# Two dense MLPs and two SwiGLU feed-forwards on one core: a reciprocal, down blocks, weight splits and parts of x in another order

## The chip, the cores and the metric

The kernel runs on one core of one Trainium2 chip. The metric is the device time of one execution in microseconds (us); the number compared is the median of several runs. TensorE (PE) multiplies, VectorE (DVE) and ScalarE (ACT) work on the tiles, GpSimd (POOL) adds and issues a few transfers, and SyncE (SP) issues nearly all of them.

## What is computed

Everything is float32, for 512 tokens of 1024 features. Two transformer blocks come first (stick-breaking attention, then retention, each with an MLP behind it), then a third block whose feed-forwards stand ahead of and behind a mixer of sparse attention and mLSTM:

```python
for layer in range(2):
    h = h + mixer(rms_norm(h, g_mix[layer]))            # stick-breaking, then retention
    u = relu(rms_norm(h, g_mlp[layer]) @ w_mlp_up[layer])   # 1024 -> 4096
    h = h + (u * u) @ w_mlp_down[layer]                 # 4096 -> 1024
x = rms_norm(h, g_final)
# second block, D_FF = 2816
x = x + 0.5 * (silu(n(x) @ w_gate) * (n(x) @ w_up)) @ w_down    # ffn1
x = x + mix(rms_norm(x, mix_norm)) @ w_out
x = x + 0.5 * (silu(n(x) @ w_gate) * (n(x) @ w_up)) @ w_down    # ffn2
```

Retention splits its projection into q and k (256 a head), v and a gate (512 a head) and scales the value rows by 1/rms of their token.

## The kernel before, in words

**Precision.** Each float32 factor is split in two numbers that TensorE takes at full rate: `w_hi` is a rounded copy by ScalarE (`split_hi`, L835), `w_lo = raw - w_hi` by VectorE (`split_lo`, L1684), and likewise `x_hi`/`x_lo` and `u_hi`/`u_lo`. A product is three matmuls: w_hi with x_hi, w_hi with x_lo, w_lo with x_hi.

**Blocks.** A weight block is 1024 by 128, read by one 512 KB transfer into one of two `raw` slots. Block n uses slot n % 2 of `raw`, `w_hi` and `w_lo`, and a PSUM bank. TensorE starts block n when `hi_done` says that w_hi is there and `bank_free` that the bank's last product was read; 16 matmuls with w_hi (L2834) are followed by 8 with w_lo (L2839). w_hi of block n + 2 can be made when block n is done (`mm_done`), and block n + 2 is loaded when split_lo(n) has read the slot (`lo_done`).

**MLPs (layers 0 and 1).** The first 8 up blocks are dense (`mlp`, c = 0 to 7). VectorE reads the product into `u_act` (L2034), which frees its bank; ScalarE squares it and makes `u_hi`; VectorE makes `u_lo`. The factor 1/rms isn't in u: it is squared (`inv_sq`) and multiplied in with the down products. Besides, each c makes parts for later: `x_forms` are sums and differences of halves of x (`x_sum`, split into `xs_hi`, `xs_lo`).

**Pairs.** The other up columns, and in layers 2 and 3 (ffn1, ffn2) gate and up, are made in pairs of blocks by a Strassen-like scheme of 7 units (q, p), p = 1 to 7, each 12 matmuls of 256 columns (L3133 with the high part of a form, L3137 with the low). The forms of pair q lie in `forms[q % 2]`: four transfers by SP (`load_forms`, L746, L749, L752, L755), a fifth by GpSimd that adds a block onto two of them (L2790), and two sums by VectorE (`third_form` L1942, `fourth_form` L1947). `form_high` (L1037) and `form_low` (L1935) split each form into a ring of four. Units 1 and 6 are copied by ScalarE (`first_copy`, `second_copy`, L1044); unit 4 adds onto the bank of 7 and waits until `last_copy` (L2075) has read it. `up_phase` sets the order of the units: in the first phase of a feed-forward it is (q0,5), (q0,1), (q0,2), (q0,6), (q0,7), (q1,1), (q0,4), (q0,3), (q1,2), (q1,6), ... Units 1, 2 and 4 read x itself; in layers 2 and 3 that is the normed x, in four parts, which `x_normed_high` (L1215) and `x_normed_low` (L2176) write over `x_hi` and `x_lo` once the last dense block has read them.

**Down blocks.** The hidden chunks are taken in groups of 8 (in a feed-forward 8, 8, 6). `up_and_down` lays the first two down blocks n and n + 1 of a group among the last units, chunk by chunk as u becomes ready (`down_part`, L3146); the other six follow as dense blocks (`run`).

**Queues.** Every engine works through its own list in the order of the code; SP does too, so a transfer waits for those written ahead of it. At the start TensorE turns x into columns, with 24 empty transposes (`keep_awake`) in between.

## Time and profile before

| | us |
|---|---|
| median of 3 runs | 2423.54 (2421.94 to 2423.86) |
| the profiled execution, its own time | 2422.37 |
| its span, first to last instruction | 2420.5 |
| PE busy | 2397.0 (99%) |
| DVE busy | 1625.4 (67%) |
| ACT busy | 1156.2 (48%) |
| POOL busy | 154.7 (6%) |

The chain of work that ended last lies for 90% of the span on PE, and the granted PE clock is full in each of the 40 slices of the page. So the time changes only where PE's idle time does: a row's bracket, [idle before <-releaser], says how long an engine was idle ahead of an instruction and what ended it.

### The profile page before, as it was taken

The page shows a single profiled execution, that of the slowest core. Times are in us where ns is not written, and L with a number is a line of the kernel's source. Part 1 is how long each engine was busy: PE and PEld are TensorE (multiplying, and loading weights), DVE is VectorE, ACT ScalarE, POOL GpSimd, SP SyncE. Part 2 cuts the span into 40 slices and gives each one's busy share as a digit, 9 for nine tenths or more (in the row PEclk, how much of TensorE's full clock was granted, in tenths as well). Part 3 has the DMA queues.
Part 4 walks back from the last instruction along what each step waited for, and adds up shares of the span by engine and source line. Part 5 has one row for each costly group of instructions (what it writes and reads, how often), then busy time and mean ns, then how long its engine had stood idle before and what let it go on. Part 6 is the DMA issues. An engine that isn't in the chain of part 4 may idle for free.

```text
span 2420.5 us, 35737 instructions
## 1 busy us (share of the span) xinstructions
PE 2397.0 (99%) x13500; PEld 2063.5 (85%) x13500; DVE 1625.4 (67%) x2386; ACT 1156.2 (48%) x1837; POOL 154.7 (6%) x151
## 2 busy tenths in 40 slices
PE   9999999999999999999999999999999999999999
PEld 7777798998888888789998889898787778889998
DVE  6777765666656646756666967676968846867664
ACT  3565544554343443535645535354465453544443
POOL 2001000001000000100003000002000001000000
PEclk9999999999999999999999999999999999999999
DMA  4212443533222223445541555552222222555552
GB/s 140 68 64 70 148 148 106 156 105 106 95 79 81 76 79 96 134 136 138 149 131 61 158 147 167 139 157 85 79 70 70 70 70 96 151 154 164 142 154 82
DMA packets 108194, 273.50 MB, mean 113 GB/s; under 512 B 15120, under 2 KB 33808, under 8 KB 107920
## 3 DMA queue, kind: packets, MB, share of 16 engines
q1 hardware_dynamic: 95168, 237.98, 29.6%
q0 software_dynamic: 8640, 31.46, 7.8%
q10 hardware_dynamic: 4240, 2.10, 0.3%
q8 instruction: 94, 1.54, 0.3%
q14 instruction: 52, 0.43, 0.1%
HBM read 269.40 MB, written 2.10 MB: 112 GB/s over the span
## 4 chain that ended last, share of the span: by engine, by line
PE 90%; DVE 5%; issue 2%; ACT 1%; DMA 1%; POOL 1%; DVEq 0%; SPq 0%; ACTq 0%; POOLq 0%
PE ps L2834 29%; PE ps L3133 16%; PE ps L2839 14%; PE ps L3137 8%; PE ps L3146 6%; PE ps L3213 4%; PE ps L2887 2%; PE ps L3514 2%; PE ps L2903 2%; PE ps L3256 1%; PE ps L3038 1%; PE ps L3014 1%; PE ps L2991 1%; PE ps L3243 1%; DVE w_lo L1684 1%
## 5 line engine op out<-in xcount | busy, mean ns | idle before, releaser
L835 ACT ACTIVATE w_hi<-raw 128x1024 fp32r<-128x1024 f32 x286 | 302.4, 1059 | 771.2 <-PE ps L2839 584.5
L1684 DVE TENSOR_TENSOR w_lo<-raw,w_hi 128x1024 fp32r<-128x1024 f32 x286 | 352.1, 1231 | 118.5 <-ACT w_hi L835 118.1
L2834 PE MATMUL ps<-x_hi,w_hi 128*128 128x512 f32 x848 | 337.4, 398 | 4.8 <-DVE u_act L2034 4.4
L2834 PE MATMUL ps<-x_lo,w_hi 128*128 128x512 f32 x848 | 330.6, 390 | 0.0
L2834 PE MATMUL ps<-u_hi,w_hi 128*128 128x512 f32 x642 | 250.8, 391 | 2.8 <-ACT w_hi L835 2.8
L2834 PE MATMUL ps<-u_lo,w_hi 128*128 128x512 f32 x642 | 249.9, 389 | 0.0
L3133 PE MATMUL ps<-xs_hi,ring 128*128 128x256 f32 x960 | 240.8, 283 | 1.3 <-ACT second_copy L1044 1.3
L3133 PE MATMUL ps<-xs_lo,ring 128*128 128x256 f32 x960 | 240.7, 283 | 0.0
L1037 ACT ACTIVATE ring<-forms 128x512 fp32r<-128x512 f32 x300 | 187.7, 628 | 87.8 <-PE ps L3137 85.8
L2839 PE MATMUL ps<-x_hi,w_lo 128*128 128x512 f32 x848 | 209.5, 389 | 0.0
L2834 PEld LDWEIGHTS ps<-x_hi,w_hi 128*128 128x128 f32 x848 | 159.2, 188 | 45.6 <-issue 11.0
L2834 PEld LDWEIGHTS ps<-x_lo,w_hi 128*128 128x128 f32 x848 | 159.3, 188 | 33.5 <-issue 1.7
L2839 PEld LDWEIGHTS ps<-x_hi,w_lo 128*128 128x128 f32 x848 | 159.2, 188 | 33.1
L3133 PEld LDWEIGHTS ps<-xs_hi,ring 128*128 128x128 f32 x960 | 184.2, 192 | 1.7 <-issue 1.7
L3133 PE MATMUL ps<-x_hi,ring 128*128 128x256 f32 x720 | 180.9, 284 | 3.6 <-DVE x_lo L2176 1.8
L3133 PEld LDWEIGHTS ps<-xs_lo,ring 128*128 128x128 f32 x960 | 184.3, 192 | 0.1
L3133 PE MATMUL ps<-x_lo,ring 128*128 128x256 f32 x720 | 180.6, 283 | 0.0
L2839 PE MATMUL ps<-u_hi,w_lo 128*128 128x512 f32 x642 | 159.0, 389 | 0.0
L1935 DVE TENSOR_TENSOR ring_b<-forms,ring 128x512 fp32r<-128x512 f32 x224 | 152.3, 682 | 4.1 <-ACT ring L1037 3.9
L2834 PEld LDWEIGHTS ps<-u_hi,w_hi 128*128 128x128 f32 x642 | 120.5, 188 | 29.7 <-DVE h L1837 4.9
L3133 PEld LDWEIGHTS ps<-x_hi,ring 128*128 128x128 f32 x720 | 138.0, 192 | 5.5 <-issue 3.0
L1837 DVE SCALAR_TENSOR_TENSOR h<-ps,h 128x512 f32<-128x512 f32 (+1 forms) x71 | 49.0, 690 | 138.7 <-PE ps L2839 116.4
(476 smaller groups left out, 4653.5 us busy)
## 6 DMA issues: line engine op xcount, KB each, us to landing
raw<-in_stream SPq DMA_DIRECT2D x293, 512.0 KB, 3.6
forms<-in_stream SPq DMA_DIRECT2D x180, 256.0 KB, 4.4
forms<-in_stream SPq DMA_DIRECT2D x60, 512.0 KB, 4.7
forms<-in_stream POOLq DMA_DIRECT2D x60, 512.0 KB, 5.7
x_tok<-in_x SPq DMA_DIRECT2D x4, 512.0 KB, 8.0
out_x<-xn ACTq DMA_DIRECT2D x7, 256.0 KB, 2.3
tab_ret<-in_tables_ret SPq DMA_DIRECT2D x1, 1536.0 KB, 6.6
raw<-in_stream SPq DMA_DIRECT2D x3, 256.0 KB, 3.2
```

The source lines that it names most:

```text
L835: nc.scalar.activation(w_hi[:, slot(n)], raw[:, slot(n)], ACT.Copy).then_inc(hi_done, 1)
L1037: nc.scalar.activation(form_hi[form_slot(v)], form_of(q, p), ACT.Copy).then_inc(flag("f_hi"), 1)
L1684: nc.vector.tensor_tensor(w_lo[:, slot(n)], raw[:, slot(n)], w_hi[:, slot(n)].bitcast(F32), ALU.subtract).then_inc(lo_done, 1)
L1837: nc.vector.scalar_tensor_tensor(out=dst, in0=product(n), scalar=scale, in1=dst, op0=ALU.mult, op1=ALU.add).then_inc(bank_free[slot(n)], 1)
L1935: nc.vector.tensor_tensor(form_lo[form_slot(v)], form_of(q, p), form_hi[form_slot(v)].bitcast(F32), ALU.subtract).then_inc(flag("f_lo"), 1)
L2834: nc.tensor.matmul(ps[:, gemm_bank(n)], w_hi[:, s, k], x(k), start=(k == 0 and i == 0), stop=False)
L2839: last = nc.tensor.matmul(ps[:, gemm_bank(n)], w_lo[:, s, k], hi(k), start=False, stop=(k == kc - 1))
L2887: return nc.tensor.transpose(dst, src, ident)
L3133: nc.tensor.matmul(bank, form_hi[s][:, j * P:(j + 1) * P], x_part(p, j, i == 0), start=(p in (1, 2, 5) and j == 0 and i == 0), stop=False, ...
L3137: last = nc.tensor.matmul(bank, form_lo[s][:, j * P:(j + 1) * P], x_part(p, j, True), start=False, stop=(j == 3), skip_group_check=True)
L3146: last = nc.tensor.matmul(ps[:, gemm_bank(n)], w[:, slot(n), k], x[:, 0, k], start=(k == 0 and i == 0), stop=(k == kc - 1 and i == 2))
L3213: return nc.tensor.matmul(ps[:, RET_BANKS[tb]], x[:, c, tb * P:(tb + 1) * P], weights, start=(c == 0 and w is w_hi and x is x_hi), stop=(c ...
```

## The change

It has seven parts: (1) the reciprocal of an MLP's norm, and its square, are made behind up block 5 instead of block 0; (2) at the end of each group of a feed-forward, PE finishes down block n ahead of all chunks from 4 on of block n + 1; (3) the splits of these two blocks' weights, ahead of units (q0,3) and (q1,6) before, stand at (q1,6) and (q2,6), and one set of forms is loaded between the loads n and n + 1; (4) VectorE makes the first three low parts of the normed x ahead of the fourth low form and `fourth_form`, and ScalarE the fourth high part at unit 5 instead of unit 6; (5) retention's first value block waits for `first + 2` and `first + 3` in place of `first + 4` and `first + 5`; (6) the first gains are loaded by ScalarE's queue; (7) ScalarE splits weight block 0 ahead of the second chunk of x.

```diff
@@ SP, start
             load_x(0)
-            sp.dma_start(prm[:, 0:DC], params[:, 0:DC]).then_inc(sig("gain_in"), 16)
             load_values(0)
@@ SP, load_layer
                     load(n)
+                    if layer >= 2 and g == 0:
+                        load_forms(qs[1] + 2)
                     load(n + 1)
                     for q in qs:
-                        if q + 2 < PAIR_FROM[layer + 1] and (layer < 2 or g or q > qs[0]):
+                        if q + 2 < PAIR_FROM[layer + 1] and (layer < 2 or g or q > qs[1]):
                             load_forms(q + 2)
@@ ACT, start
+            nc.scalar.dma_start(prm[:, 0:DC], params[:, 0:DC]).then_inc(sig("gain_in"), 16)
             nc.scalar.preload_act_table_set("sqrt_and_others")
             act.wait_ge(sig("gain_in"), 16)
             high_of(N_MIX0, 0)
+            split_hi(0)
             high_of(N_MIX0, 1)
-            split_hi(0)
@@ ACT, gate_pairs
-                    if g == 0 and (q, p) == (qs[0], 6):
+                    if g == 0 and (q, p) == (qs[0], 5):
                         x_normed_high(layer, 3)
...
-                    if g == 0 and (q, p) in ((qs[0], 3), (qs[1], 6)):
-                        split_hi(RUN_AT[LAYERS[layer]] + 2 * FFN_DENSE + q - qs[0])
+                    if g == 0 and (q, p) in ((qs[1], 6), (qs[2], 6)):
+                        split_hi(RUN_AT[LAYERS[layer]] + 2 * FFN_DENSE + q - qs[1])
@@ DVE, mlp
                     split_lo(n + 2)
-                    if c == 0:
-                        inverse(norm)
-                        nc.vector.tensor_tensor(inv_sq[:], inv[:], inv[:], ALU.mult).then_inc(flag("down_scaled"), 2)
                     dve.wait_ge(sig("uh_done"), chunks_before + c + 1)
                     nc.vector.tensor_tensor(u_lo[:, 0, c], u[:, c % 2], u_hi[:, 0, c].bitcast(F32),
                                             ALU.subtract).then_inc(sig("ul_done"), 1)
+                    if c == 5:
+                        inverse(norm)
+                        nc.vector.tensor_tensor(inv_sq[:], inv[:], inv[:], ALU.mult).then_inc(flag("down_scaled"), 2)
@@ DVE, gate_pairs
-                    if g == 0 and (q, p) in ((qs[0], 3), (qs[1], 6)):
-                        split_lo(RUN_AT[LAYERS[layer]] + 2 * FFN_DENSE + q - qs[0])
+                    if g == 0 and (q, p) in ((qs[1], 6), (qs[2], 6)):
+                        split_lo(RUN_AT[LAYERS[layer]] + 2 * FFN_DENSE + q - qs[1])
@@ DVE, ffn
                         third_form(PAIR_FROM[layer])
-                        form_low(v)
-                        form_low(v + 1)
-                        fourth_form(PAIR_FROM[layer])
-                        form_low(v + 2)
-                        form_low(v + 3)
+                        for i in range(3):
+                            form_low(v + i)
                         for i in range(3):
                             x_normed_low(layer, i)
+                        form_low(v + 3)
+                        fourth_form(PAIR_FROM[layer])
@@ PE, up_and_down
                     if layer < 2:
                         down_part(n, made, (kc - 2,), kc)
-                    else:
-                        down_part(n + 1, made, range(4, kc - 1), kc)
                     down_part(n, made, (kc - 1,), kc)
-                    down_part(n + 1, made, range(4 if layer < 2 else kc - 1, kc), kc)
+                    down_part(n + 1, made, range(4, kc), kc)
@@ PE, retention
-            pe.wait_ge(bank_free[0], turn(first + 4, 1))
-            pe.wait_ge(bank_free[1], turn(first + 5, 1))
+            pe.wait_ge(bank_free[0], turn(first + 2, 1))
+            pe.wait_ge(bank_free[1], turn(first + 3, 1))
```

Each value block waits besides, in `r_value_block`, for `bank_free` of its own slot: the first for `turn(first + 4, 1)`, the second for `turn(first + 5, 1)`. These lines are not changed.

On VectorE, in the MLP of layer 0, between up blocks 0 and 1, the kernel before has this:

```order
L2034 TENSOR_SCALAR u_act<-ps 128x512
L1684 TENSOR_TENSOR w_lo<-raw,w_hi 128x1024
L1719 RECIPROCAL inv<-std 128x512
L2038 TENSOR_TENSOR inv_sq<-inv 128x512
L2040 TENSOR_TENSOR u_lo<-u,u_hi 128x512
L1878 TENSOR_TENSOR xs_lo<-x_sum,xs_hi 128x1024
```

With the change these two instructions stand at the end of block 5 (lines are those of the changed file):

```order
L2036 TENSOR_SCALAR u_act<-ps 128x512
L1686 TENSOR_TENSOR w_lo<-raw,w_hi 128x1024
L2039 TENSOR_TENSOR u_lo<-u,u_hi 128x512
L1721 RECIPROCAL inv<-std 128x512
L2043 TENSOR_TENSOR inv_sq<-inv 128x512
L2036 TENSOR_SCALAR u_act<-ps 128x512
```

So nothing stands any more between w_lo and u_lo of block 0, and the two instructions stand ahead of the read of block 6.

On TensorE, at the end of the first group of layer 2, the kernel before goes, ahead of the dense down blocks (the group of four is chunks 0 to 3 of block n + 1):

```order
L3146 MATMUL ps<-u_hi,w_lo 128x512 x4
L3146 MATMUL ps<-u_hi,w_hi 128x512 x3
L3146 MATMUL ps<-u_lo,w_hi 128x512 x3
L3146 MATMUL ps<-u_hi,w_lo 128x512 x3
L3146 MATMUL ps<-u_hi,w_hi 128x512
L3146 MATMUL ps<-u_lo,w_hi 128x512
L3146 MATMUL ps<-u_hi,w_lo 128x512
L3146 MATMUL ps<-u_hi,w_hi 128x512
L3146 MATMUL ps<-u_lo,w_hi 128x512
L3146 MATMUL ps<-u_hi,w_lo 128x512
```

And with the change:

```order
L3147 MATMUL ps<-u_hi,w_lo 128x512 x4
L3147 MATMUL ps<-u_hi,w_hi 128x512
L3147 MATMUL ps<-u_lo,w_hi 128x512
L3147 MATMUL ps<-u_hi,w_lo 128x512
L3147 MATMUL ps<-u_hi,w_hi 128x512 x4
L3147 MATMUL ps<-u_lo,w_hi 128x512 x4
L3147 MATMUL ps<-u_hi,w_lo 128x512 x4
```

Before, three chunks of block n + 1 (9 matmuls), the last chunk of block n (3) and the last of block n + 1 (3); now the last chunk of block n at once, and four chunks of block n + 1 (12) behind it. In the groups of 6 chunks the 9 matmuls are 3.

On VectorE, at the end of the dense part of layer 2, where the ring gets the first four low forms, the kernel before has:

```order
L1942 TENSOR_TENSOR form_sum<-forms_80 128x512
L1935 TENSOR_TENSOR ring<-forms_80,ring 128x512
L1935 TENSOR_TENSOR ring_b<-forms_80,ring 128x512
L1947 TENSOR_TENSOR form_sum<-forms_80,form_sum 128x512
L1935 TENSOR_TENSOR ring_b<-forms_80,ring 128x512
L1935 TENSOR_TENSOR ring_b<-form_sum,ring 128x512
L2176 TENSOR_TENSOR x_lo<-x_even,x_hi 128x2x256 x2
L2176 TENSOR_TENSOR x_lo<-x_odd,x_hi 128x4x256
L1696 SCALAR_TENSOR_TENSOR u<-ps,inv 128x512
```

With the change:

```order
L1944 TENSOR_TENSOR form_sum<-forms_80 128x512
L1937 TENSOR_TENSOR ring<-forms_80,ring 128x512
L1937 TENSOR_TENSOR ring_b<-forms_80,ring 128x512 x2
L2178 TENSOR_TENSOR x_lo<-x_even,x_hi 128x2x256 x2
L2178 TENSOR_TENSOR x_lo<-x_odd,x_hi 128x4x256
L1937 TENSOR_TENSOR ring_b<-form_sum,ring 128x512
L1949 TENSOR_TENSOR form_sum<-forms_80,form_sum 128x512
L1698 SCALAR_TENSOR_TENSOR u<-ps,inv 128x512
```

The three x_lo instructions moved up past two others; what follows them is where it was.

## Rows read from the trace of the kernel before

**Rows 1.** The page: busy time, share of the span and instructions of each engine

```profile
PE 2397.0 (99%) x13500; PEld 2063.5 (85%) x13500; DVE 1625.4 (67%) x2386; ACT 1156.2 (48%) x1837; POOL 154.7 (6%) x151
```

**Rows 2.** Waits of PE over the span: total us, times, longest

```profile
PE ps L2834 <- DVE u_act L2034: 4.4, 2, 2.3
PE ps L2834 <- ACT w_hi L835: 3.2, 6, 0.6
...
PE ps L3133 <- DVE last_copy L2075: 1.7, 2, 0.9
...
PE ps L3137 <- DVE ring_b L1935: 0.2, 1, 0.2
PE ps L2887 <- DVE h L1837: 0.2, 1, 0.2
```

**Rows 3.** Timeline, MLP of layer 0: start, us, engine, line, tiles, [idle before]

```profile
255.92 3.35 DVE L1719 RECIPROCAL inv<-std 128x512 f32<-128x512 f32 x1 [1.98 <-ACT std L888]
256.44 0.63 ACT L1134 ACTIVATE u_hi<-u 128x512 fp32r<-128x512 f32 x1
...
259.99 0.68 DVE L2040 TENSOR_TENSOR u_lo<-u,u_hi 128x512 fp32r<-128x512 f32 x1
...
265.90 1.97 PE L2839 MATMUL ps<-x_hi,w_lo 128*128 128x512 f32 x8
...
269.32 0.68 DVE L2034 TENSOR_SCALAR u_act<-ps 128x512 f32<-128x512 f32 x1
...
270.15 0.47 PE L2834 MATMUL ps<-x_hi,w_hi 128*128 128x512 f32 x1 [2.28 <-DVE u_act L2034]
```

**Rows 4.** Timeline, the first down block of layer 0: its weights and first matmuls

```profile
288.74 1.06 ACT L835 ACTIVATE w_hi<-raw 128x1024 fp32r<-128x1024 f32 x1 [5.11 <-DMA raw<-in_stream]
...
292.01 1.07 PE L3146 MATMUL ps<-u_hi,w_hi 128*128 128x512 f32 x4
```

**Rows 5.** Timeline of TensorE and VectorE, end of a group in layer 2

```profile
1420.65 0.42 DVE L2083 TENSOR_TENSOR u<-ps,second_copy 128x256 f32<-128x256 f32 x1 [2.58 <-PE ps L3137]
...
1422.50 0.69 DVE L2097 TENSOR_TENSOR u_lo<-u,u_hi 128x512 fp32r<-128x512 f32 x1 [0.70 <-ACT u_hi L1170]
...
1428.09 2.01 ACT L835 ACTIVATE w_hi<-raw 128x1024 fp32r<-128x1024 f32 x2 [5.62 <-PE ps L3146]
...
1429.28 0.49 PE L2834 MATMUL ps<-u_hi,w_hi 128*128 128x512 f32 x1 [0.55 <-ACT w_hi L835]
```

**Rows 6.** Timeline, second pair of layer 2: a weight split and unit 4

```profile
1392.00 1.22 DVE L1684 TENSOR_TENSOR w_lo<-raw,w_hi 128x1024 fp32r<-128x1024 f32 x1
...
1395.50 0.36 PE L3133 MATMUL ps<-x_hi,ring 128*128 128x256 f32 x1 [0.85 <-DVE last_copy L2075]
```

**Rows 7.** Timeline, third pair of layer 2: its last_copy, and a form that waits

```profile
1399.04 0.33 SPq L746 DMA_DIRECT2D forms<-in_stream  x1
...
1404.50 0.42 DVE L2075 COPY last_copy<-ps 128x256 f32<-128x256 f32 x1 [0.75 <-PE ps L3137]
...
1408.52 0.69 DVE L1942 TENSOR_TENSOR form_sum<-forms 128x512 f32<-128x512 f32 x1 [2.54 <-DMA forms<-in_stream]
```

**Rows 8.** Timeline, layer 3, the first parts of the normed x

```profile
2105.94 1.14 ACT L1215 ACTIVATE x_hi<-x_even 128x512 fp32r<-128x512 f32 x2
...
2107.35 0.68 DVE L1935 TENSOR_TENSOR ring_b<-form_sum,ring 128x512 fp32r<-128x512 f32 x1
...
2107.95 1.28 DVE L2176 TENSOR_TENSOR x_lo<-x_even,x_hi 128x512 fp32r<-128x512 f32 x2
...
2108.78 0.36 PE L3133 MATMUL ps<-x_hi,ring 128*128 128x256 f32 x1 [1.53 <-DVE x_lo L2176]
```

**Rows 9.** Timeline, retention: the first value block

```profile
611.13 1.17 PE L3213 MATMUL ps<-w_hi,x_hi 128*128 128x512 f32 x4 [1.09 <-DVE r_x L1696]
```

**Rows 10.** Timeline, the start: the gains' transfer and the first real matmuls

```profile
1.68 0.50 SPq L721 DMA_DIRECT2D prm<-in_params  x1
...
9.60 2.12 PE L2903 MATMUL ps<-w_hi,x_hi 128*128 128x512 f32 x8
```

## The prediction

> **What bounds the kernel now.** I read the page first: PE is busy for 2397.0 us of a span of 2420.5 [rows 1], and the granted clock is full throughout. No work is removed, so at most the idle 23.5 us and what hides beside them are to be had. Then the list of what PE waited for: the reader is to see that few waits are long and that five of them are the subject of the change [rows 2]. Then the timeline around each of these, PE beside VectorE and ScalarE [rows 3 to 9]: which engine is late, and what stands ahead of the late instruction in its list.
>
> One reading is needed for the prices. A row of eight matmuls is 1.97 us long [rows 3] and one alone 0.39, so they start 0.226 apart, and each row covers 0.16 us beyond the next start. In the MLP the last of eight starts at 265.90 + 1.97 - 0.39 = 267.48, the next matmul at 270.15: 2.67, less the normal 0.226, is 2.44 us lost, where the idle column says 2.28 [rows 3]. So a stall costs its idle time plus 0.16. The Trainium skill (Perfetto Trace Analysis, Identifying the Most-Contended Engine) says that matmul occupancy is no good measure for TensorE since its instructions are pipelined. By idle times alone the sum below would be some 2 us smaller; the trace agrees with the page through the 0.16.
>
> **The change part by part.**
>
> (1) Reciprocal in the MLPs. It waits 1.98 us for std and takes 3.35, then the square follows, and only then u_lo of block 0, at 259.99, though its u_hi was there at 256.44 + 0.63 = 257.07 [rows 3]. u_lo moves to 257.1, 2.9 us earlier. Behind it come xs_lo, four sums and the reads of blocks 1 and 2, all VectorE's own chain or ScalarE's answer to it, so the read of block 2 (269.32) starts near 266.45 and ends at 267.1. PE wants that bank at 267.7: the stall goes, with 0.6 to spare. Layer 1 has the second of the two waits of 4.4 us [rows 2], 2.1 idle. Gain 4.4 + 2 x 0.16 = 4.7. The reciprocal's new place: PE wants the bank of block 6 again when block 7 is done, two blocks of 24 x 0.226 = 5.4 us behind block 5. u_lo of block 5 ends about 3 us behind its product (read, square, high and low part at 0.6 to 0.7 each), so 7.8 us are left for reciprocal, square and read, 3.35 + 0.7 + 0.7 = 4.8; hidden. With less cover each missing microsecond would cost one. Next late is the weight of the first down block: w_hi starts on a DMA landing at 288.74 and w_lo is ready some 1.06 + 1.22 later, at 291.0, against PE at 292.01, now 289.5 [rows 4, 6]. Its transfer stands behind eight loads of forms, which stand behind a load that waits for the split of block 5. That split moves 2.9 earlier with the chain, the split of block 6 by about 2.6, and so the transfer by the same; I take slack as kept. The other bound is that it doesn't move at all: 1.6 lost a layer.
>
> (2) End of a feed-forward group. w_hi of block n + 2 can't be made until block n is done; it starts at 1428.09, and PE starts at 1429.28 after 0.55 idle [rows 5]. Of the six waits for w_hi [rows 2] five are at the ends of such groups: four like this one, and that of the group of 6 chunks, which is the longest with 0.6. 4 x 0.55 + 0.6 + 5 x 0.16 = 3.6; the sixth lies elsewhere and stays. Block n is now done 9 matmuls earlier in the groups of 8, 9 x 0.226 = 2.0 us, more than the 0.71; in the group of 6 it is 3 x 0.226 = 0.68 of its 0.77. In the first group of layer 2 the bank comes next: its read stands behind a reciprocal, I leave 0.1 for that. Gain 3.6 - 0.2 = 3.4. The last group ends with PE's wait for h, 0.2 idle [rows 2]; 0.68 is more than its 0.36: gained whole. Together 3.75. What speaks against it: the last chunk's u_lo is now wanted 2.0 us earlier. The last six matmuls and the nine ahead of them begin 14 x 0.226 before 1428.34 (1429.28 less the idle 0.55 and a row of 0.39), at 1425.2; u_lo ends at 1422.50 + 0.69 = 1423.2 [rows 5]. 2.0 us are left, so hidden.
>
> (3) Splits and forms. PE waits 0.85 for last_copy at 1395.50, as VectorE has two weight splits of 1.22 each within four microseconds, one at 1392.00 [rows 6]. The first of them leaves. VectorE has then caught up and is only as late as PE's product of unit 7 allows, which is 0.3 us or more ahead of the wait. Both waits for last_copy go: 1.7 + 2 x 0.16 = 2.0 [rows 2]. The other split goes to the third pair, where last_copy at 1404.50 has 0.75 us idle ahead of it [rows 7] and the ring is ahead: 1.22 against 0.75 makes last_copy 0.5 late, about what lies between last_copy and PE's wait for it. I take nothing; the other bound is 0.5 a layer. SP: a load now waits for the split at the third pair, 84 matmuls of 256 columns behind the one at 1392.00, some 9 us, near 1402.3 at its end, and the forms that had been issued at 1399.04 stand behind it [rows 7], 3.7 us later. That helps the set before, whose added part reached VectorE at 1408.52 only, 2.54 late [rows 7]; PE's 0.2 behind it goes, 0.2 + 0.16 = 0.4. For the later set I reckon its landing at about the old time, since the same bytes wait for fewer; VectorE has 2.58 us idle behind the place where it wants it [rows 5].
>
> (4) x parts. In layer 3 x_hi is there from 2105.94 + 0.57 on (two in 1.14), but x_lo starts at 2107.95 behind two instructions that move behind it, 0.60 start to start each (2107.35 to 2107.95) [rows 8]. 1.2 us earlier is 2106.75, still behind x_hi. PE's 1.53 + 0.16 shrinks by 1.2. In layer 2 VectorE is ready before x_hi, and moving the rest changes nothing. The next four low forms and fourth_form are 1.2 later; the copies behind them wait for PE longer than that. Gain 1.2. ScalarE's fourth part at unit 5 instead of 6 frees second_copy by 0.1 at most: nothing.
>
> (5) Retention. PE waits 1.09 us for r_x [rows 9], the read of block first + 3, but the first value block's own wait asks only for the bank of first + 2, read a block earlier. The wait moves behind 24 matmuls, 5.4 us, and goes: 1.09 + 0.16 = 1.25.
>
> (6, 7) Start. PE works without idle time up to its first real matmuls at 9.60 [rows 10], since the empty transposes end just then; an earlier block 0 gains nothing. SP saves 0.50 us of issue [rows 10]. Between 0 and 0.5 lost if the small transfer on its own queue delays the first ones; I take 0.
>
> Sum: 4.7 + 3.75 + 2.0 + 0.4 + 1.2 + 1.25 = 13.3. The profiled execution took 2422.37, so 2409.1; it lies 1.2 below the median, and 2423.54 - 13.3 = 2410.2.
>
> **The rivals.**
>
> All as summed, 0.66: 2410.2, its own range 2408 to 2412.5.
>
> Down weights late in the MLPs, 0.12. The transfers there are many, and the landing may hold at 288.74 [rows 4]. Then PE, at 289.5, waits until 291.1: 1.6 of layer 0's gain goes and about as much of layer 1's, 2410.2 + 3 = 2413.2. For it: w_hi waits 5.11 us for that DMA. Against: what it waits behind moves with it.
>
> The moved split and the later forms make new stalls, 0.09. 0.3 to 0.5 a layer at the third pair and about 1 a layer where the added form lands beyond the 2.58: 2413.
>
> The gains' transfer delays the start, 0.05. PE's first transposes want the first part of x; if that comes 0.5 later, all does, 2410.7. The Trainium skill (DMA: Bandwidth & Descriptors, Issuing engines are not separate DMA queues; Queues, rings and completion order) says that transfers of all engines share 16 DMA engines, which take turns between queues, and that another queue only saves issue time. No row here shows the split.
>
> The change only hands the stalls on, 0.06. w_hi early but the bank late at group ends, and half of every gain back at the next wait: 2416.9. Against it speak the slacks worked out above, each over 0.3.
>
> Slower than before, 0.02: the forms issued after 1399.04 come so late that the hidden chunk behind third_form stops PE. It decides only once the landing is late by more than VectorE's 2.58, the 2.0 that u_lo has, and half the sum, 6.7, in each of two layers: 11 us, where the issue moves by 3.7. One more microsecond makes 2426.
>
> **Range and chances.** A difference under 0.2%, 4.8 us, can't be told from none here. 2407.5 to 2415 takes in the first four cases with the unknown bounds (0.5 at the start, 0.5 a layer at the splits, 3 at the weights) and leaves out the last two. All but the slower case and the upper half of the fifth lie below 2418.7: faster 0.95, same 0.03, slower 0.02.
>
> **What would show it.** PE's list of waits without u_act, with w_hi at 0.5 us or less in total, last_copy and r_x gone, x_lo at about 0.6; u_lo of block 0 in the MLP right behind its u_hi, the reciprocal behind block 5. PE's idle time near 12 us. Wrong would make it: a wait of PE for w_hi or w_lo of the first down blocks, one for a bank at the group ends, or for u_lo of the last chunk, or the first x later than before.

## The result, and the profile after

| us | before | after |
|---|---|---|
| median, runs of the first comparison | 2423.7 (4: 2421.94 to 2424.52) | 2407.44 (4: 2407.14 to 2407.99) |
| the profiled execution, its own time | 2422.37 | 2407.99 |
| its span | 2420.5 | 2406.2 |

The ratio is 0.9932, interval 0.9918 to 0.9945: faster by 0.7%, that is by 16.3 us in the medians and by 14.4 in the two profiled executions. The forecast was 2410.2, with a range of 2407.5 to 2415.0. The sign and the places were right; the size was 2.8 us short, and the result lies 0.06 us below the range.

The page of the changed kernel, its line of busy times, answers to [rows 1]:

```profile
PE 2393.8 (99%) x13500; PEld 2063.6 (86%) x13500; DVE 1627.7 (68%) x2386; ACT 1157.2 (48%) x1837; POOL 155.1 (6%) x151
```

TensorE is idle for 2406.2 - 2393.8 = 12.4 us, where it was 23.5; the forecast said near 12. Its list of waits (total us, times, longest) answers to [rows 2]:

```profile
PE ps L3134 <- ACT second_copy L1046: 1.1, 2, 0.6
...
PE ps L3134 <- DVE x_lo L2178: 0.6, 2, 0.4
PE ps L2835 <- DVE h L1839: 0.5, 1, 0.5
...
PE ps L2835 <- ACT w_hi L836: 0.3, 1, 0.3
```

The lines of the kernel before that [rows 2] does not show:

```profile
PE ps L3133 <- DVE x_lo L2176: 1.8, 2, 1.5
PE ps L3133 <- ACT second_copy L1044: 1.3, 2, 0.7
...
PE ps L3213 <- DVE r_x L1696: 1.1, 1, 1.1
```

u_act, last_copy, r_x and ring_b are gone, w_hi is down from 3.2 to 0.3, x_lo from 1.8 to 0.6, second_copy from 1.3 to 1.1. New is the 0.5 for a sum of h: one of the forecast's signs of being wrong, a bank that is late at a group end, has come in one group. The MLP of layer 0 (timeline of VectorE and TensorE, against [rows 3]):

```profile
256.67 0.69 DVE L2039 TENSOR_TENSOR u_lo<-u,u_hi 128x512 fp32r<-128x512 f32 x1 [3.17 <-ACT u_hi L1136]
...
260.08 0.68 DVE L2036 TENSOR_SCALAR u_act<-ps 128x512 f32<-128x512 f32 x1
...
265.46 1.98 PE L2840 MATMUL ps<-x_hi,w_lo 128*128 128x512 f32 x8
267.27 0.39 PE L2835 MATMUL ps<-x_hi,w_hi 128*128 128x512 f32 x1
...
281.30 3.35 DVE L1721 RECIPROCAL inv<-std 128x512 f32<-128x512 f32 x1
284.75 0.69 DVE L2043 TENSOR_TENSOR inv_sq<-inv 128x512 f32<-128x512 f32 x1
285.36 0.69 DVE L2036 TENSOR_SCALAR u_act<-ps 128x512 f32<-128x512 f32 x1
```

u_lo of block 0 stands right behind its u_hi, TensorE goes from block to block at 267.27 with no idle time, and the reciprocal in its new place ends, with the read of block 6 behind it, at 286.05. TensorE wants that bank only with the matmul at 289.04, behind the eight that begin at 287.22, so 3.0 us are left, as forecast (7.8 less 4.8).

To see where the time came from I compared, over the whole program, the start of the k-th matmul in both traces. This difference, the lead of the changed kernel, grows in steps: 0.46 us from the first real matmul on, 2.54 and 2.43 in the two MLPs, 1.37 at retention's values, 1.07 and 1.09 at last_copy of layers 2 and 3, 0.48 at the form of layer 2, 0.08 and 1.18 at the x parts, and at the ends of the six groups 0.03, 0.84, 0.67, 0.84, 0.84 and 0.43. Together 14.35.

The end of the first group of layer 2 (timeline, against [rows 5]) has the 0.03:

```profile
1411.65 0.69 DVE L1944 TENSOR_TENSOR form_sum<-forms 128x512 f32<-128x512 f32 x1 [3.52 <-DMA forms<-in_stream]
...
1412.86 0.42 DVE L2085 TENSOR_TENSOR u<-ps,second_copy 128x256 f32<-128x256 f32 x1
...
1415.91 3.35 DVE L1721 RECIPROCAL inv_final<-std_final 128x512 f32<-128x512 f32 x1
...
1417.64 1.06 ACT L836 ACTIVATE w_hi<-raw 128x1024 fp32r<-128x1024 f32 x1 [2.97 <-PE ps L3147]
...
1420.08 0.69 DVE L1839 SCALAR_TENSOR_TENSOR h<-ps,h 128x512 f32<-128x512 f32 x1
...
1420.82 0.50 PE L2835 MATMUL ps<-u_hi,w_hi 128*128 128x512 f32 x1 [0.50 <-DVE h L1839]
```

w_hi is there at 1418.70, two microseconds early, as forecast. But VectorE waited 3.52 us for the late forms, so the reciprocal begins late and the read of the bank behind it ends at 1420.77.

### The profile page after: what moved, and what is told of

Its sections match the earlier page's. It is cut to its first block, busy times and chain, and to the rows that moved or that the text cites. A ratio compares the mean times of both kernels' runs of the same rounds, so it can differ in the third digit from the quotient of the medians.

```text
span 2406.2 us, 35737 instructions
## 1 busy us (share of the span) xinstructions
PE 2393.8 (99%) x13500; PEld 2063.6 (86%) x13500; DVE 1627.7 (68%) x2386; ACT 1157.2 (48%) x1837; POOL 155.1 (6%) x151
## 4 chain that ended last, share of the span: by engine, by line
PE 92%; DVE 4%; issue 2%; ACT 1%; DMA 1%; POOL 1%; SPq 0%; ACTq 0%; DVEq 0%; POOLq 0%
PE ps L2835 29%; PE ps L3134 16%; PE ps L2840 14%; PE ps L3138 8%; PE ps L3147 6%; PE ps L3212 4%; PE ps L3513 2%; PE ps L2904 2%; PE ps L2888 2%; PE ps L3255 1%; PE ps L3039 1%; PE ps L3015 1%; PE ps L2992 1%; PE ps L3242 1%; DMA forms<-in_stream 1%
## 5 line engine op out<-in xcount | busy, mean ns | idle before, releaser
L2840 PEld LDWEIGHTS ps<-u_hi,w_lo 128*128 128x128 f32 x642 | 120.5, 188 | 25.0
L2835 PEld LDWEIGHTS ps<-u_lo,w_hi 128*128 128x128 f32 x642 | 120.5, 188 | 24.9
```

Of the source, the lines that this page charges most:

```text
L2835: nc.tensor.matmul(ps[:, gemm_bank(n)], w_hi[:, s, k], x(k), start=(k == 0 and i == 0), stop=False)
L2840: last = nc.tensor.matmul(ps[:, gemm_bank(n)], w_lo[:, s, k], hi(k), start=False, stop=(k == kc - 1))
```

## Experiments

Times below are medians; where the runs of one kernel fall into groups, the single runs are given. A lead is always that of TensorE over the kernel before, read matmul by matmul from two traces. The kernel before was timed 75 times beside these experiments.

### First set: a control and three parts alone

**e1_null**: no edit but a comment.

> The kernel before, unchanged in every instruction. It measures the measurement: the runs of the kernel before lie between 2421.94 and 2424.52 us, those of the changed one within 0.9 us. Theory A (the trace accounts for 14.3 us of the gain, and the 2 us that the medians show beyond it are scatter of the kernel before from run to run): ratio 1.000 within 0.0006, single runs scattered over some 2.5 us here too. Theory B (the kernel before has, in its other runs, waits that its profiled execution did not have, and the change removes them): the same scatter here, and then a single part below must give more by its timed runs than its two traces account for.

Measured: 2423.06 against 2423.42, ratio 0.9996 (0.9987 to 1.0005), 11 runs from 2421.44 to 2424.20. Each run also has the granted clock of TensorE as a mean over the span: the five fastest have 1.000, the six from 2423.06 on 0.999. The scatter of the kernel before goes with the clock. Its trace also leads that of before, the same kernel, by 0.40 us from the form of layer 2 on and loses 0.33 at a form of layer 3: the wait of 0.2 us for ring_b in [rows 2] is one outcome, not a fixed cost.

**e2_reciprocal**:

```diff
-                    if c == 0:
+                    if c == 5:   # behind u_lo of the block
                         inverse(norm)
                         nc.vector.tensor_tensor(inv_sq[:], inv[:], inv[:], ALU.mult)
```

> Part 1 alone. By the forecast's pricing, a stall costs its idle time plus 0.16 us: 4.7 us. By the traces of before and after, in which the lead of TensorE grows by 2.54 and 2.43 us in the two MLPs, a stall costs its idle time plus 0.27 us: 5.0 us, ratio 0.9979. If the down weights come late (the rival of the forecast) it is 1.6 us less a layer. Waits of TensorE: none for u_act, the rest as before.

Measured: 2417.20 against 2423.42, 6.2 us, ratio 0.9974 (0.9964 to 0.9985). Its trace leads that of before by the expected 2.54 and 2.41 in the MLPs, and by 0.26 at the form of layer 2, which is scatter as in e1. So the timed gain is 1.2 us more than the two steps account for, and the scatter shrinks: 8 runs within 1.3 us, all at a clock of 1.000, where 30 runs of before spread over 3.7.

**e3_down_blocks**:

```diff
-                    if layer < 2:
-                        down_part(n, made, (kc - 2,), kc)
-                    else:
-                        down_part(n + 1, made, range(4, kc - 1), kc)
+                    if layer < 2:
+                        down_part(n, made, (kc - 2,), kc)
                     down_part(n, made, (kc - 1,), kc)
-                    down_part(n + 1, made, range(4 if layer < 2 else kc - 1, kc), kc)
+                    down_part(n + 1, made, range(4, kc), kc)
```

> Part 2 alone. The forecast says 3.75 us. With 0.27 us for a stall in place of 0.16 and with the first group of layer 2 gaining nothing (its bank comes next: with all parts in, TensorE waits there 0.50 us for a sum of h that stands behind a reciprocal) it is 0.84 x 3 + 0.7 + 0.4, about 3.5 us, ratio 0.9986. If parts 3 and 2 depend on each other (the reciprocal's place is set by the read of the pair before), the first group of layer 2 gains here what it did not gain with all parts in: 4.2 us.

Measured: 2419.33, 4.1 us, ratio 0.9982 (0.9973 to 0.9991); steps of the lead 0.64, 0.85, 0.67, 0.84, 0.84, 0.43, so 4.3. The first group of layer 2 gains 0.64 here and 0.03 with all parts in: another part takes it back.

**e4_gains_by_scalar_queue**:

```diff
-            sp.dma_start(prm[:, 0:DC], params[:, 0:DC]).then_inc(sig("gain_in"), 16)
+            nc.scalar.dma_start(prm[:, 0:DC], params[:, 0:DC]).then_inc(sig("gain_in"), 16)
```

> Part 6 alone. In the changed kernel TensorE leads by 0.46 us from its first blocks on; the forecast took 0 for parts 6 and 7. Theory: the 0.50 us of issue that SyncE is spared brings all tokens behind it earlier, so this part alone gives 0.46 us and part 7 nothing. Rival: the earlier split of weight block 0 (part 7) gives it, and this part alone gives 0 to 0.1 us.

Measured: 2423.21, ratio 1.0000 (0.9991 to 1.0009): nothing that such scatter lets through. Its trace tells more. TensorE's wait for u_act is the same 2.28 us, but what follows isn't (timeline of TensorE, and a table of stretches: start and end, length, PE busy, granted clock, DMA share, GB/s):

```profile
269.88 0.49 PE L2834 MATMUL ps<-x_hi,w_hi 128*128 128x512 f32 x1 [2.28 <-DVE u_act L2034]
270.19 0.61 PE L2834 MATMUL ps<-x_lo,w_hi 128*128 128x512 f32 x1
270.60 0.63 PE L2834 MATMUL ps<-x_hi,w_hi 128*128 128x512 f32 x1
271.02 0.63 PE L2834 MATMUL ps<-x_lo,w_hi 128*128 128x512 f32 x1
...
273.58 0.41 PE L2834 MATMUL ps<-x_lo,w_hi 128*128 128x512 f32 x1
273.83 0.39 PE L2834 MATMUL ps<-x_hi,w_hi 128*128 128x512 f32 x1
```

```profile
266.00:270.00 4.00, 1.72 (x9) 1.00 0.41 131
270.00:274.00 4.00, 4.00 (x11) 0.57 0.41 128
274.00:278.00 4.00, 4.00 (x19) 1.00 0.47 153
```

There are 11 matmuls in the middle four microseconds and 19 in the four behind them. From 270.19 to 273.58 they start (273.58 - 270.19) / 8 = 0.424 us apart, against 0.227 elsewhere: TensorE is at 1.2 GHz of its 2.4. That costs 8 x 0.2 = 1.6 us, and no column of idle time has it, since the engine counts as busy: the lead falls by 1.62 here. The Trainium skill (TensorE: Matmul & The Clock Gate, What's actually happening) says that the clock has these two states; its section Wait — 56ns, not 53.3ns? gives 426.7 ns start to start for 512 columns in the slow one, and the trace agrees with 424. In e3 the same happened behind the same wait; in the profiled executions of before and of e1 it did not.

### Second set: is it the clock?

**e5_fillers_in_the_wait**:

```diff
                 for i in range(1, blocks):
+                    if i == 4 and layer < 2:
+                        for j in range(16):
+                            turn_block(ps[:, 3, j % TB * P:(j % TB + 1) * P], ident)
                     of_x(first + i, ...)
```

> The kernel before with nothing moved, but 16 empty transposes of 128x128 (some 0.11 us each, 1.75 in all) on TensorE at the head of its wait for u_act, ahead of up block 4 of both MLPs. In two of four traces of kernels that still have this wait, the eight matmuls behind the 2.28 us of idle start 0.427 us apart at a granted clock of 0.57 over their stretch, in the others 0.23 apart at 1.00: 1.6 us. And 30 timed runs of the kernel before lie in three heaps, 12 at 2421.6 to 2422.8, 12 at 2423.1 to 2424.0 and 6 at 2424.9 to 2425.3, as none, one or two such drops would give. Theory C (the scatter is this drop, and the idle time brings it): the wait ends at the same time as before, idle time shrinks to some 0.5 us, no run lies in the upper heaps, so all within 1.3 us around 2422.2, the median 1.2 below before, and no stretch below 1.00 behind the fillers. Rival D (the scatter is from elsewhere, transfers say, and the drop an accompaniment): three heaps as before, median 2423.4. Rival E (the reciprocal's move gave the extra microsecond by what it does on VectorE): as D.

Measured: 2422.80 against 2423.67, 11 runs from 2421.77 to 2423.42, every one at a clock of 1.000; of the 21 runs of before beside them 13 were at 0.999 and reached 2426.16. Its TensorE:

```profile
267.37 1.91 PE L2887 MATMUL ps<-tab 128*128 128x128 f32 x16
269.80 0.47 PE L2834 MATMUL ps<-x_hi,w_hi 128*128 128x512 f32 x1 [0.53 <-DVE u_act L2034]
```

The wait ends as it did, only its idle part is filled, and no run has a lower clock. VectorE does exactly what it did before, so D and E fall, and theory C stands. It shows in the clock and in the spread (1.65 us against 4.5) more than in the median: that is 0.9 lower, where 1.2 was expected, and the five slowest runs, 2423.00 to 2423.42, reach into the middle heap in time, though at a clock of 1.000. The mean, 2422.74, lies 0.5 above that of the runs of the kernel before at a clock of 1.000 (2422.23); that half microsecond is not explained.

**e6_reciprocal_layer0**:

```diff
-                    if c == 0:
+                    if c == 0 and norm == N_MLP1:   # layer 1 as before
...
+                    if c == 5 and norm == N_MLP0:   # layer 0 as changed
```

> Part 1 in the MLP of layer 0 alone; layer 1 keeps its wait of 2.15 us. Theory C: two heaps 1.6 us apart instead of three, the lower at 2422.2 - 2.55 = 2419.65, the upper at 2421.3, none above 2421.8. Rival D: three heaps, 2419.7 to 2422.7.

Measured: 2419.95, ratio 0.9987 (0.9977 to 0.9996). Ten runs: seven at 1.000 from 2419.18 to 2420.35, three at 0.999 from 2421.06 to 2421.47. There are two heaps instead of three: one such wait gives one possible drop.

**e7_split_block0_first** (a single run):

```diff
             high_of(N_MIX0, 0)
+            split_hi(0)
             high_of(N_MIX0, 1)
-            split_hi(0)
```

> Part 7 alone. With part 6 alone, and with neither, TensorE waited 0.4 to 1.1 us for the w_hi of block 0 ahead of its first real matmul in four traces, so that split, not the empty transposes, sets the start. Theory: this part alone brings the first real matmul forward by one high part of x, some 0.3 to 0.5 us against the kernel before; rival: it needs part 6 as well and gives 0 to 0.1 alone.

Measured: 2422.39, and its first real matmul at 9.93, later than in any trace so far, because the first part of x landed late (TensorE waited 0.75 us for it). Not settled by this run.

**e8_splits_and_forms** (a single run; part 3 alone, of which this is the half on the splits, on ScalarE and VectorE; the other half are the pieces of SP in load_layer):

```diff
-                    if g == 0 and (q, p) in ((qs[0], 3), (qs[1], 6)):
+                    if g == 0 and (q, p) in ((qs[1], 6), (qs[2], 6)):
```

> Part 3 alone. The forecast says 2.4 us by idle plus 0.16 a stall; with 0.27 a stall for the two last_copy waits and the form's 0.2 it is 2.6: 1.08 and 1.09 us at last_copy in layers 2 and 3, 0.4 at the form in layer 2. Rival (the waits for last_copy go with the earlier x parts, part 4, as much as with the splits): under 1.5 us here.

Measured: the clock dropped in both MLPs (1.60 and 1.59 us lost), so its 2423.29 says little, but the steps of its trace do: 1.05 and 1.06 at last_copy, 0.47 at the form, and -0.48 at the end of the first group of layer 2, 2.1 in all. The rival, under 1.5 us, falls. The 0.47 can't be booked to part 3 as a whole: e1, e4, e7 and e13, which don't have it, lead by 0.40 to 0.49 at the same form, and e1, e4 and e7 lose 0.15 to 0.41 at a form of layer 3. The forms ahead of that (timeline of GpSimd and VectorE):

```profile
1412.27 0.86 POOL L2792 DMA_DIRECT2D forms<-in_stream  x1 [9.98 <-DMA forms<-in_stream]
...
1422.07 0.69 DVE L1944 TENSOR_TENSOR form_sum<-forms 128x512 f32<-128x512 f32 x1 [4.02 <-DMA forms<-in_stream]
...
1423.29 0.42 DVE L2085 TENSOR_TENSOR u<-ps,second_copy 128x256 f32<-128x256 f32 x1
```

In the kernel before the same transfer was issued here:

```profile
1408.96 0.86 POOL L2790 DMA_DIRECT2D forms<-in_stream  x1 [7.63 <-DMA forms<-in_stream]
```

e8 runs 1.5 us behind before at this point, so GpSimd's adding transfer goes out 1412.27 - 1408.96 - 1.5 = 1.8 us later, because the transfers by SP that it waits for land later, and form_sum starts 9.8 us behind that issue. VectorE is 4.02 us idle, more than the 2.58 of [rows 5], and everything behind it on VectorE, the reciprocal and the read of the bank, is late.

### Third set: with the scatter gone, parts by leaving them out

Kernels without the waits for u_act have little scatter, so a single part can be timed by taking it out of the changed kernel. Reference is that kernel's nine runs: 2406.61 to 2407.99, median 2407.23.

**e9_after_again**: no edit.

> The changed kernel again, on one chip with the next three, so that they can be compared. By theory C none of its waits is long enough for the clock to drop, so all runs at a clock of 1.000 within some 1.2 us around 2407.5, against a kernel before in two to three heaps. If any run is above 2408.7, another wait drops the clock too.

Measured: 2406.95, 5 runs from 2406.61 to 2407.96, all at 1.000. In its trace one wait is new (timelines of the three engines, the first down block of layer 1):

```profile
1023.29 1.06 ACT L836 ACTIVATE w_hi<-raw 128x1024 fp32r<-128x1024 f32 x1 [6.20 <-DMA raw<-in_stream]
1024.38 1.23 DVE L1686 TENSOR_TENSOR w_lo<-raw,w_hi 128x1024 fp32r<-128x1024 f32 x1 [1.91 <-ACT w_hi L836]
1025.87 0.94 PE L3147 MATMUL ps<-u_hi,w_hi 128*128 128x512 f32 x3 [0.24 <-DVE w_lo L1686]
```

This is the forecast's rival of the down weights, in layer 1 alone and small: 0.24 us idle, 0.52 of lead, where the rival had 1.6 a layer. Of the eight traces of the changed kernel and its variants one more shows it (e10, 0.35 of lead). In layer 0 the weights came earlier with the chain, as the forecast took it: the w_lo that started at 289.83 starts at 285.96.

**e10_without_start_parts** (parts 6 and 7 undone):

> The changed kernel without parts 6 and 7: gains by SyncE's queue, weight block 0 split behind the second chunk of x. In the one pair of traces the changed kernel led by 0.46 us from the start on, but the start of ten traces with and without these parts lies anywhere between 0.31 later and 0.25 earlier than in the kernel before. If the lead is real this is 0.4 to 0.5 us slower than the changed kernel, 2407.9; if it is scatter of the start, the same within 0.15 us. The forecast took 0.

Measured: 2407.98, 0.75 above the reference and 1.0 above e9 on the same chip, five runs from 2407.60 to 2408.99. The start of its trace:

```profile
4.90 1.97 PE L2888 MATMUL ps<-tab,x_tok 128*128 128x128 f32 x8 [0.22 <-DMA x_tok<-in_x]
6.66 2.06 PE L2888 MATMUL ps<-tab 128*128 128x128 f32 x16
9.41 1.89 PE L2904 MATMUL ps<-w_hi,x_hi 128*128 128x512 f32 x7 [0.70 <-ACT w_hi L835]
```

The empty transposes take 2.06 us here and end early, and TensorE waits for w_hi of block 0. Over all traces the first real matmul starts at 9.33 to 9.73 in nine kernels without both parts (median 9.46), with a wait for that w_hi in five of them, and with both at 8.76 to 9.36 in six kernels (median 9.18), never with that wait; in a seventh (e16) it is at 10.51, as the first part of x came 0.7 us late. So the start gives about 0.3 us by the traces and 0.75 to 1.0 by the runs, whose ranges overlap, under a scatter of its own. Where the first real matmul is later than 9.6, the first part of x landed late (e6, e7, e16).

**e11_without_splits_and_forms** (part 3 undone):

> The changed kernel without part 3. It loses 1.08 + 1.08 us at last_copy and gets back what part 3 takes at the end of the first group of layer 2: with part 3 alone in, form_sum there waits 4.02 us for its forms instead of not at all, the reciprocal is 1.5 us later and the group ends 0.48 us later, and the down blocks' part gave 0.64 us there without part 3 and 0.03 with it. So 2.16 + 0.4 - 0.6, about 1.9 us slower than the changed kernel. If the forms' delay costs nothing (the forecast's step), 2.6 us slower.

Measured: 2410.57, 3.3 above the reference, five runs from 2409.49 to 2411.23. By its trace against e9 it is 2.66, in these steps: 1.32 and 1.33 around last_copy in layers 2 and 3, 0.23 and 0.40 at the forms behind it, less 0.11 in the first group of layer 2, where form_sum doesn't wait, and less 0.52 at the down weights of layer 1, where only e9 waited. TensorE at last_copy:

```profile
1387.26 0.74 PE L3136 MATMUL ps<-x_hi,ring 128*128 128x256 f32 x4
1388.89 0.35 PE L3132 MATMUL ps<-x_hi,ring 128*128 128x256 f32 x1 [0.89 <-DVE last_copy L2075]
```

With part 3 out of the changed kernel last_copy costs 0.25 more than in the kernel before, and most of that is in two matmuls ahead of the wait that start 0.1 late each. So part 3 is worth more beside the other parts than alone (1.05 in e8); the later low forms of part 4 would explain it, but that wasn't tested by itself. My 1.9 was too low for this reason and because I had taken the cost of the late forms as certain, where in e9 it is 0.1. The alternative, 2.6, has the right sum by luck: its terms are others.

**e12_reciprocal_in_the_gap**:

```diff
                 if more:
                     form_low(v + 2)
+                    if layer == 2 and g == 0:
+                        inverse(N_FINAL)
                     third_form(q + 1)
...
                     elif g == 0 and norm == N_FFN1:
-                        inverse(N_FINAL)
                         residual_of_final(n, 0.5)
```

> The changed kernel with one instruction moved: in layer 2 VectorE takes the reciprocal of the final norm (3.35 us) while it waits 3.5 us for the late forms at the end of the first group, instead of behind the pair's last work. Theory: the bank of the first dense down block is then read in time, TensorE's 0.50 us for that sum of h goes, 0.66 us less: 2406.8 against 2407.5. Rival: w_hi of that block, made by ScalarE at 1417.64, or its w_lo behind the same reciprocal is as late as the bank, and nothing or at most 0.2 us comes back.

Measured: 2406.64, five runs from 2406.43 to 2407.11, 0.3 below e9 on the same chip and 0.6 below the nine. VectorE and TensorE at the place (timeline):

```profile
1407.45 3.35 DVE L1721 RECIPROCAL inv_final<-std_final 128x512 f32<-128x512 f32 x1
1410.83 0.69 DVE L1944 TENSOR_TENSOR form_sum<-forms 128x512 f32<-128x512 f32 x1
...
1417.12 0.69 DVE L1839 SCALAR_TENSOR_TENSOR h<-ps,h 128x512 f32<-128x512 f32 x1 [1.27 <-PE ps L3148]
```

The reciprocal now fills the wait for the forms, the read of the bank waits for TensorE instead of the other way round, and TensorE's wait for h is gone from its list; the step of the lead at this group is 0.83 instead of 0.03. The rival falls. In time it is 0.3 to 0.6 where 0.66 was expected, and the ranges of the runs overlap, so only the trace shows it clear of scatter. Less than 0.66 fits with what the changed kernel and its variants gain at this group from trace to trace: 0.03, 0.54 (e9), -0.32 (e10), 0.65 (e14) and 0.35 (e15).

### Fourth set: how long a wait, and the other parts

**e13_square_later** (kernel before, only inv_sq behind block 5):

```diff
                     if c == 0:
                         inverse(norm)
-                        nc.vector.tensor_tensor(inv_sq[:], inv[:], inv[:], ALU.mult)
...
+                    if c == 5:
+                        nc.vector.tensor_tensor(inv_sq[:], inv[:], inv[:], ALU.mult)
```

> The kernel before with only the square of the reciprocal moved behind up block 5, the reciprocal itself where it was. The wait of TensorE for u_act shrinks from 2.28 to some 1.6 us (the square takes 0.61 start to start) in both MLPs, 2 x 0.61 = 1.2 us. Theory C1 (the drop of the clock comes with the length of the wait and is gone for shorter ones): all runs at a clock of 1.000 around 2422.2 - 1.2 = 2421.0. Theory C2 (any wait of this kind can bring it): some runs at 0.999, heaps 1.6 us apart, 2421.0, 2422.6, 2424.2, median 2422.2.

Measured: 2420.49 against 2423.09, 2.6 us, all eleven runs at 1.000, ten of them from 2420.03 to 2421.33 (one at 2422.91). By its trace the two waits cost 0.79 and 0.69 less, 1.5. So an instruction of 0.69 us moved twice gave 1.1 us on top, the price of the drop, which came behind none of these shorter waits:

```profile
268.96 0.47 PE L2835 MATMUL ps<-x_hi,w_hi 128*128 128x512 f32 x1 [1.48 <-DVE u_act L2034]
269.27 0.40 PE L2835 MATMUL ps<-x_lo,w_hi 128*128 128x512 f32 x1
269.50 0.40 PE L2835 MATMUL ps<-x_hi,w_hi 128*128 128x512 f32 x1
```

The three rows also show what every stall costs beyond idle time plus 0.16: the second matmul starts 0.31 behind the first and not 0.227, and the next ones 0.23, about 0.1 in all. Theory C1 stands, C2 falls; where between 1.48 and 2.15 us the drop begins to come isn't measured.

**e14_without_retention_part**, **e15_without_x_parts**, **e16_without_down_part** (part 5, 4 or 2 undone):

> The changed kernel without part 5. The traces give the part 1.37 us (the forecast 1.25): 2408.5 against 2407.1 to 2407.5. If its wait of 1.09 us also drops the clock in some runs, runs at 2410 with a clock of 0.999 appear; if not, all at 1.000 within 1.2 us.

> The changed kernel without part 4. By the traces 1.17 us in layer 3 and about 0.1 in each of the two layers at second_copy: 1.3 us, 2408.6. The forecast said 1.2 and nothing at second_copy.

> The changed kernel without part 2. By the traces 0.84 + 0.67 + 0.84 + 0.84 + 0.43 = 3.6 us and up to 0.6 in the first group of layer 2, where the late forms take it back in some runs: 3.6 to 4.2, so 2410.9 to 2411.5. The forecast said 3.75.

Measured: 2408.46, 2408.50 and 2411.13, so 1.2, 1.3 and 3.9 above the reference, five runs each, all at 1.000. These three ran on another chip than e9, and no run of the changed kernel stands beside them, so some tenths can be the chip's. The wait of 1.09 us (e14) brought no drop in these five runs, nor in the 8 of e2 and 11 of e13, which have it too.

## Why the prediction was right or wrong

| part | forecast | steps of the lead | timed |
|---|---|---|---|
| 1 reciprocal | 4.7 | 4.97 | 6.2 (e2, put in alone) |
| 2 down blocks | 3.75 | 3.65 | 3.9 (e16) |
| 3 splits and forms | 2.4 | 2.64 | 3.3 (e11) |
| 4 x parts | 1.2 | 1.26 | 1.3 (e15) |
| 5 retention | 1.25 | 1.37 | 1.2 (e14) |
| 6, 7 start | 0 | 0.46 | 0.75 (e10) |
| sum | 13.3 | 14.35 | 16.65 |

The steps of the lead are from the trace of the changed kernel against that of before. The timed parts add up to more than the 16.1 to 16.3 of the whole; each of them has a scatter of some half a microsecond, and part 3 is worth more beside the others than alone (e8, e11).

**The mechanisms held.** All five stalls were ended by what the forecast named and went as it said, the slacks it worked out were there (reciprocal behind block 5, u_lo of the last chunk), and none of the waits were handed on whole. TensorE's idle time fell to 12.4 us, as forecast.

**The step that failed: the median minus the sum.** The forecast saw that the profiled execution lay 1.2 us below the median and carried this on as a constant by taking the sum, read from one execution, off the median. In the changed kernel the profiled execution lies 0.55 above the median. This step gives 1.7 of the 2.8 us that were missed, and the sum of the parts, 13.3 against 14.4 in the traces, the other 1.1. What the 1.2 stood for is the clock: of 75 runs of the kernel before, 32 had a clock of 1.000, with a mean of 2422.23, and 43 a lower one, with a mean of 2424.19; the mean of all is 2423.35. The drop of the clock behind the two waits for u_act therefore costs 1.1 us in the mean run and nothing in the one that was profiled, and it goes with the waits. e2, e5, e6 and e13 show it. At 1.6 us a drop, 1.1 is 0.7 drops a run or 0.35 a wait, and the three dropped runs of ten with one such wait (e6) agree. The other 0.6 of the 1.7 is where the two profiled executions lie among the runs of their kernels without a drop; that was luck, here bad. The range took in no such term, since every stall was priced from one execution, and no term of the forecast is behind its lower end of 2407.5.

**The term that was mis-sized: 0.16 for a stall.** The forecast counted only the overlap of two matmuls. The first matmuls behind a stall are also further apart, as the rows of e13 show, and a stall costs its idle time plus 0.26 to 0.28. 0.3 of this shows in the reciprocals, 0.1 in retention and 0.2 in part 3; the 0.6 of part 2's six stalls is used up by the late forms, below.

**The form of layer 2, 0.4.** The step was there (0.48), but in part by luck: the same kernel without a change (e1) has it at 0.40 against the profiled execution, and pays 0.33 in layer 3. In the other traces without part 3 such waits fall partly in layer 2 and partly in layer 3 (e4: all in layer 3, 0.41).

**Start, taken as 0.** "An earlier block 0 gains nothing" rested on one execution in which TensorE had no idle time ahead of 9.60 [rows 10]. That was one outcome of several: in five of nine traces of such kernels TensorE waits for w_hi of block 0. The two parts together are worth 0.3 (starts of the first real matmul) to 0.75 or 1.0 (runs of e10); which of them gives it e4 and e7 didn't settle.

**The forms, "landing at about the old time".** The issue by SP moved by 4.4 us (in the changed kernel 1395.51 plus a lead of 7.9, against 1399.04) where the forecast had 3.7: its 84 matmuls of 256 columns, 0.12 us apart, take 10.1 us and not 9. Nor did the landing stay: GpSimd's adding transfer, which waits for it, went out 1.8 us later (e8), and its reader follows 8.3 to 9.8 us behind that. The forecast had not followed this second transfer. In e8 VectorE waits 4.02 us for it and in the changed kernel 3.52, more than its cover of 2.58 [rows 5], so the first group of layer 2 gains 0.65 in one execution (e14), 0.03 in another and -0.32 in a third (e10), where the forecast had 0.6 (0.55 + 0.16 - 0.1). It was one of the rivals (chance 0.09), at the right place and priced too high: 1 us a layer, where it is up to 1 in layer 2 and nothing in layer 3. e12 takes it away, and the term comes back: its step of the lead there is 0.83.

**Sum of the two readings.** By means 2423.35 - 2407.27 = 16.1 us. The clock gives 1.1 of it, the two traces 14.4, and the last 0.6 is that the profiled execution of the changed kernel lies 0.7 above the mean of its nine runs and that of before 0.1 above its undropped ones. What sets those last tenths is, as far as the traces show, the landing of the first part of x (TensorE waits for it between not at all and 0.75 us), of the forms, and of the down weights of layer 1 (up to 0.52 us). I did not test it by itself; the cause of this part stays open.

## What to carry to other kernels

Ask of the longest stalls of TensorE not only how long they are, but whether the clock behind them stays up, and ask it of several executions, as one profile shows one outcome: medians minus a profiled time can hide such a term, and then it leaves with the stall. Price a stall from the start-to-start distances of the matmuls on both sides, not from the idle column. Where a moved transfer feeds a second transfer (here GpSimd's add), follow both before calling it hidden, and put long work without deadline into the wait that is left, as e12 did.

## What the runs showed of the hardware

- Behind waits of TensorE of 2.28 and 2.15 us its granted clock fell to half in some executions, for 8 to 9 matmuls of 512 columns 0.424 us apart, 1.6 us a time; by the mean clock 43 of 75 runs with these two waits had at least one such drop (the traces with a mean of 0.999 show one or two, those with 1.000 none). With waits of 1.48 us in their place it fell in none of 11 runs (e13), behind the 1.09 of retention in none of 24 (e2, e13, e14), and with 16 transposes laid into the 2.28 in none of 11 (e5).
- A first matmul of 512 columns behind idle time takes 0.47 to 0.50 us instead of 0.39, and the second starts 0.31 behind it instead of 0.227.
- The start of a program varies by more than a microsecond: the first real matmul began between 8.76 and 10.51 us in seven traces of kernels with the same start.
- An adding transfer of 512 KB by GpSimd (L2791 or L2792) had its reader start 8.3 us (e9), 8.9 us (changed kernel) and 9.8 us (e8) behind its issue.
